# A split-precision decoder kernel: three products of 288 columns per contraction step and half, replaced for the first 256 tokens by one product of 512 columns and one of 256

## The reference, cut to what matters

```
x  -> mixer -> y;   h = x + rmsnorm(y @ w_out) * g_mix_post
u  = rmsnorm(h) @ w_ffn_up                     # 1024 -> 5632
c  = depthwise causal conv of width 3 over u
y  = (gelu(gate) * val) @ w_ffn_down           # 2816 -> 1024
h  = h + rmsnorm(y) * g_ffn_post
h  = h + rmsnorm(sigmoid(h @ w_ple_gate) * (p @ w_ple_proj)) * g_ple
```

## Time and profile before

| | |
|---|---|
| median of 3 runs | 2083.34 us (2082.45 to 2084.76) |
| the profiled execution's own time | 2080.89 us |
| its span | 2079.1 us |
| PE busy | 1912.2 us, 92% |
| DVE busy | 1131.7 us, 54% |
| ACT busy | 717.4 us, 35% |
| mean granted TensorE clock | 0.937 |

### The profile page before, as it was taken

The page is one execution under the profiler, slowest core; times in us unless marked ns, Lnnn a source line. Parts: engine busy times, 40 slices in busy tenths (PEclk is TensorE's granted clock), DMA queues, the critical chain, the costliest instruction groups (busy, mean ns, idle before and its releaser), DMA issues.

```text
span 2079.1 us, 34106 instructions
## 1 busy us (share of the span) xinstructions
PE 1912.2 (92%) x13244; PEld 1660.8 (80%) x13244; DVE 1131.7 (54%) x2433; ACT 717.4 (35%) x1300; POOL 13.7 (1%) x27
## 2 busy tenths in 40 slices
PE   6999889899999979999999898787799999979997
PEld 5587555798999979988489896344598999979987
DVE  7982154547777762253322395555557777762254
ACT  3211233454333342254322222444454333342252
POOL 0000000000000000000000000000000000000000
PEclk9999878899999999999999957799999999999998
DMA  4112457512222222131122310655212222222121
GB/s 165 62 43 86 159 175 275 198 42 71 92 81 81 68 102 81 55 114 62 44 88 82 110 48 10 238 205 201 82 48 72 87 86 81 68 97 83 56 81 46
DMA packets 77851, 204.12 MB, mean 98 GB/s; under 512 B 12530, under 2 KB 14754, under 8 KB 77218
## 3 DMA queue, kind: packets, MB, share of 16 engines
q1 hardware_dynamic: 75442, 189.70, 27.0%
q0 software_dynamic: 2288, 12.72, 1.7%
HBM read 190.81 MB, written 10.40 MB: 97 GB/s over the span
## 4 chain that ended last, share of the span: by engine, by line
PE 83%; DVE 12%; ACT 3%; issue 2%; DMA 1%; DVEq 0%; POOL 0%; ACTq 0%; POOLq 0%
PE psum L395 39%; PE psum L559 12%; PE psum L1491 6%; PE psum L403 5%; PE psum L2034 3%; PE psum L1235 2%; PE psum L790 2%; PE psum L1210 1%; PE psum L481 1%; PE psum L1328 1%; PE psum L1305 1%; PE psum L2175 1%; DVE sb_arena_r L355 1%; PE psum L495 1%; PE psum L1060 1%
## 5 line engine op out<-in xcount | busy, mean ns | idle before, releaser
L395 PE MATMUL psum<-sb_a_sb_r,sb_ring_r 128*128 128x288 f32 x1280 | 259.1, 295 | 0.0
L395 PE MATMUL psum<-sb_a_sb_r,sb_arena_r 128*128 128x288 f32 x1280 | 257.0, 296 | 0.0
L395 PE MATMUL psum<-sb_y_sb_r,sb_arena_r 128*128 128x288 f32 x704 | 207.1, 294 | 11.4 <-DVE sb_arena_r L355 11.2
L395 PE MATMUL psum<-sb_y_sb_r,sb_ring_r 128*128 128x288 f32 x704 | 208.6, 296 | 0.0
L395 PEld LDWEIGHTS psum<-sb_a_sb_r,sb_ring_r 128*128 128x128 f32 x1280 | 206.8, 188 | 0.0
L395 PEld LDWEIGHTS psum<-sb_a_sb_r,sb_arena_r 128*128 128x128 f32 x1280 | 204.2, 188 | 0.0
L355 DVE TENSOR_TENSOR sb_ring_r<-sb_ring,sb_ring_r 128x1024 fp32r<-128x1024 f32 (+1 forms) x78 | 101.6, 1306 | 159.6 <-ACT sb_ring_r L352 158.9
L352 ACT ACTIVATE sb_ring_r<-sb_ring 128x1024 fp32r<-128x1024 f32 (+1 forms) x78 | 87.4, 1124 | 286.3 <-PE psum L395 221.2
L559 PE MATMUL psum<-sb_arena_r 128*128 128x288 f32 x960 | 160.7, 302 | 8.3 <-DVE sb_arena_r L355 8.3
L395 PE MATMUL psum<-sb_arena_r,sb_ring_r 128*128 128x288 f32 x1056 | 145.4, 299 | 20.9 <-DVE sb_arena_r L355 20.9
L395 PEld LDWEIGHTS psum<-sb_arena_r,sb_ring_r 128*128 128x128 f32 x1056 | 143.6, 192 | 21.3 <-issue 21.3
(11 more groups left out here) (420 smaller groups left out, 3415.4 us busy)
## 6 DMA issues: line engine op xcount, KB each, us to landing
sb_ring<-w SPq DMA_DIRECT2D x166, 512.0 KB, 3.5
sb_ring<-wd SPq DMA_DIRECT2D x32, 704.0 KB, 4.1
sb_arena<-sb_v SPq DMA_DIRECT2D x64, 256.0 KB, 5.4
sb_arena<-moba_v SPq DMA_DIRECT2D x56, 256.0 KB, 5.0
sb_ring<-moba_k SPq DMA_DIRECT2D x32, 256.0 KB, 4.1
sb_a_sb<-moba_k SPq DMA_DIRECT2D x32, 256.0 KB, 5.4
sb_ring<-sb_k SPq DMA_DIRECT2D x32, 256.0 KB, 4.0
sb_a_sb<-sb_k SPq DMA_DIRECT2D x32, 256.0 KB, 5.4
```

Source lines behind the costliest of these rows:

```text
L395: ins = e.eng.matmul(out[:, half, :], fr(w[p][:, k, :]), fr(x[q][:, k, cols]), start=(first and k == 0 and i == 0), stop=(last and k == kb ...
```

## The change

For each k, the tokens are cut at 256 in place of 288 (`CA`, `CW`, `COLS`). For the first 256 tokens the high and the low part of the activations are read together by one product of 512 columns with the high weights, which fills one bank: its left 256 columns hold high weights x low tokens, its right ones high x high. One product of 256 columns then adds low weights x high tokens to the right half. The other 320 tokens keep their three products, now of 320 columns. So a step of all tokens is five products in place of six, with 512 + 256 + 3 x 320 = 1728 columns, as 6 x 288 = 1728 before. ScalarE copies the right part of the bank out, and VectorE adds the left part (`dve_add_low`, and a line in `dve_up`); this addition now frees the tile. Where ScalarE took squares or a sigmoid straight from PSUM, it takes them for these tokens from SBUF behind that addition.

```diff
+CA = 256
+CW = (CA, T - CA)
-        a_sb = sb2("a_sb", KD * T)
-        y_sb = sb2("y_sb", KD * T)
+        ya_sb = sb2("ya_sb", 2 * KD * T)
+        y_sb, a_sb = ya_sb[:, 0:KD * T], ya_sb[:, KD * T:2 * KD * T]
+        def mm_first(e, bank, w, both, k, begin, end):
+            c = COLS[0]
+            wide = lambda: e.eng.matmul(psum[:, bank, :].rearrange("p (q n) -> p q n", q=2), fr(w[0][:, k, :]),
+                                        fr(both[:, :, k, c]), start=begin, stop=end)
+            low = lambda: e.eng.matmul(psum[:, bank, CA:2 * CA], fr(w[1][:, k, :]), fr(both[:, 1, k, c]),
+                                       start=False, stop=False)
+            if end:
+                low()
+                return wide()
+            wide()
+            return low()
+        def mm_second(e, bank, w, both, k, begin, end):
+            for i, (p, q) in enumerate(((0, 1), (0, 0), (1, 1))):
+                ins = e.eng.matmul(psum[:, bank, 0:CW[1]], fr(w[p][:, k, :]), fr(both[:, q, k, COLS[1]]),
+                                   start=(begin and i == 0), stop=(end and i == 2))
+            return ins
+        def mm_tokens(e, s, w, both, kb, first=True, last=True, x_parts=None, per=1):
+            for k in range(kb):
+                if x_parts is not None:
+                    e.eng.wait_ge(xl_ready, x_parts + per * (k + 1))
+                mm_first(e, 2 * s, w, both, k, first and k == 0, last and k == kb - 1)
+                ins = mm_second(e, 2 * s + 1, w, both, k, first and k == 0, last and k == kb - 1)
+            return ins
+        def act_high_out(e, dst, src):
+            e.eng.activation(dst, src, ACT.Copy).then_inc(high_out, 1)
+        def dve_add_low(e, t, dst, src):
+            e.highs += 1
+            e.eng.wait_ge(high_out, e.highs)
+            e.eng.tensor_tensor(dst, dst, src, ALU.add).then_inc(copied["dve"], 1)
...
         def act_up(e, acc):
-                        act.activation(u[:, 2:2 + HALF], psum[:, 2 * s, 0:HALF], ACT.Copy)
-                        act.activation(u[:, 2 + HALF:2 + TP], psum[:, 2 * s + 1, 0:TP - HALF], ACT.Copy)
+                        act.activation(u[:, 2:2 + TP], tokens(s)[:, 0:TP], ACT.Copy)
...
         def dve_up(e, acc, layer):
-                        v.wait_ge(copied["act"], c0 + 2 * j + w + 1 + i * RING)
+                        v.wait_ge(high_out, c0 + 2 * j + w + 1 + i * RING)
+                        v.tensor_tensor(u[:, 2:2 + CA], u[:, 2:2 + CA], psum[:, 2 * ((n0 + 2 * j + w) % 4), 0:CA], ALU.add)\
+                            .then_inc(copied["dve"], 1)
+                        v.wait_ge(copied["dve"], d0 + 2 * j + w + 1 + i * RING)
...
         def act_down(e, acc, buf):
                 wait_filled(e, t)
-                act_part_square(e, [halves(z) for z in buf], m, pair(t.s))
-                e.eng.activation(halves(a[:, m, :]), pair(t.s), ACT.Copy).then_inc(copied["act"], 1)
+                act_high_out(e, a[:, m, :], tokens(t.s))
+                e.eng.wait_ge(*t.out)
+                act_part_square(e, buf, m, a[:, m, :])
...
         def dve_layer_end(e, acc, layer):        # the gate sweep
-            for j in range(2):
+            for j in range(4):
+                dve_sweep_first(e, t[f"A{j}"], j)
+                if j < 2:
+                    dve_slab(e, gate_pairs[4 + 2 * j], 2 * j)
                 product(j, 0)
-                if j:
-                    dve_part_sum(e, gate_sums[0], 1)
-                dve_slab(e, gate_pairs[4 + 2 * j], 2 * j)
-                dve_slab(e, gate_pairs[5 + 2 * j], 2 * j + 1)
+                if j < 2:
+                    dve_slab(e, gate_pairs[5 + 2 * j], 2 * j + 1)
+                if 1 <= j < 3:
+                    dve_part_sum(e, gate_sums[0], j)
```

More of the change, by code:

```diff
@@ L439, in dve_norm, with sums @@
                 e.eng.scalar_tensor_tensor(dst[:, k, :], src[:, k, :], vcol(layer, gain, k), rstd[:, :], ALU.mult, ALU.mult)
-        COLS = (slice(0, HALF), slice(HALF, T))
-        def sums(at):
-            return [cut(at + i * T, T) for i in range(3)]
+        COLS = (slice(0, CA), slice(CA, T))
+        def sums(at, half):
+            return [cut(at + 2 * i * CW[half], 2 * CW[half]) for i in range(3)]
         def sweep_tiles(acc, pre):
             order = ["A0", "A1", "A2", "A3", "B0", "nA", "B1", "B2"] + (["pA"] if pre else []) + ["B3"]
-            return {x: acc.next("act") for x in order}
+            return {x: acc.next("dve" if x[0] == "A" else "act") for x in order}
         def act_rstd(e, t, cols, ready=None):
@@ L551, in dve_split_half, with mm_half @@
             e.parts += KD
-        def mm_half(e, out, w, x, half, x_parts=None, ks=range(KD)):
+        def mm_half(e, bank, w, both, half, x_parts=None, ks=range(KD)):
             for k in ks:
@@ L557, in mm_half @@
                     e.eng.wait_ge(xl_ready, x_parts + k + 1)
-                for i, (p, q) in enumerate(((0, 0), (0, 1), (1, 0))):
-                    ins = e.eng.matmul(out, fr(w[p][:, k, :]), fr(x[q][:, k, COLS[half]]),
-                                       start=(k == 0 and i == 0), stop=(k == KD - 1 and i == 2))
+                ins = (mm_first, mm_second)[half](e, bank, w, both, k, k == 0, k == KD - 1)
             return ins
@@ L570, in pe_sweep_unit @@
                     e.eng.wait_ge(wl_ready, e.splits)
-                last = mm_half(e, psum[:, 2 * t.s + i, 0:HALF], pairs[m], x, half, e.parts if m == 0 else None)
+                last = mm_half(e, 2 * t.s + i, pairs[m], x, half, e.parts if m == 0 else None)
             last.then_inc(acc_ready, 1)
@@ L1483, in pe_dense_split @@
                 e.eng.wait_ge(wl_ready, e.splits)
-                t = acc.next("act")
+                t = acc.next("dve")
                 wait_emptied(e, t)
-                for k in range(KD):
-                    if m == 0:
-                        e.eng.wait_ge(xl_ready, e.parts + 2 * k + 2)
-                    for half in range(2):
-                        for i, (p, q) in enumerate(((0, 0), (0, 1), (1, 0))):
-                            last = e.eng.matmul(pair(t.s)[:, half, :], fr(split[(m + off) % 4][p][:, k, :]),
-                                                fr(x[q][:, k, COLS[half]]), start=(k == 0 and i == 0),
-                                                stop=(k == KD - 1 and i == 2))
-                last.then_inc(acc_ready, 1)
+                mm_tokens(e, t.s, split[(m + off) % 4], both, KD, x_parts=e.parts if m == 0 else None, per=2)\
+                    .then_inc(acc_ready, 1)
             e.parts += 2 * KD
@@ L1499, in act_dense_split @@
             n0 = acc.n
-            for m in range(tiles):
+            done = [None] * tiles
+            for m in range(tiles + 1):
                 if m + AHEAD < tiles:
                     act_split_slab(e, m + AHEAD, n0 + m + AHEAD - 3 if m + AHEAD >= 4 else None, off)
-                t = acc.next("act")
-                wait_filled(e, t)
-                e.eng.activation(halves(dst(m)), pair(t.s), func(m)).then_inc(copied["act"], 1)
-        def dve_dense_split(e, tiles):
-            for m in range(AHEAD, tiles):
-                dve_split_slab(e, m)
+                if m < tiles:
+                    t = acc.next("dve")
+                    done[m] = t.out
+                    wait_filled(e, t)
+                    act_high_out(e, dst(m), tokens(t.s))
+                if m and func(m - 1) is not ACT.Copy:
+                    e.eng.wait_ge(*done[m - 1])
+                    e.eng.activation(dst(m - 1), dst(m - 1), func(m - 1)).then_inc(func_done, 1)
         def sp_split_first(ld):
@@ L1529, in pe_up @@
             late = acc.next("act")
-            n0, c0, w0 = acc.n, acc.count["act"], e.splits
+            n0, c0, w0 = acc.n, acc.count["dve"], e.splits
+            held = [acc.last[(n0 + j) % 4] for j in range(4)]
             def tiles(i, count):
@@ L1689, in pe_down @@
                     e.eng.wait_ge(wl_ready, e.splits)
-                    x = [z[:, 11 * part:11 * part + 11, :] for z in (ffh, ff)]
-                    last = mm_split(e, pair(t.s), dsplit[part], x, 11, first=(part == 0), last=(part == 1),
-                                    x_parts=e.parts + 11 * part if m == 0 else None)
+                    last = mm_tokens(e, t.s, dsplit[part], f_both[:, :, 11 * part:11 * part + 11, :], 11, first=(part == 0),
+                                     last=(part == 1), x_parts=e.parts + 11 * part if m == 0 else None)
                     last.then_inc(part_done if part == 0 else acc_ready, 1)
@@ L1795, in act_gate_square @@
             e.eng.wait_ge(prod_ready, e.prods)
[L1796 to L1797 removed]
+            act_part_square(e, [two(z) for z in gate_sums[half]], j, a[:, 2 * j:2 * j + 2, COLS[half]])
             if j == 3:
@@ L2120, in dve_proj_c @@
                 dve_split_slab(e, n, off=2)
+            dst = [z[:, m, :] for z, n in ((qh, 4), (kh, 4), (gh, 4), (zqk, 8)) for m in range(n)]
             for m in range(20):
```

188 lines of the change are left out of this document (108 added, 80 removed).

## The result

The changed kernel takes **2092.16 us** (median of 20 runs, 2081.93 to 2098.88), the kernel before 2084.82 us beside it (20 runs, 2080.23 to 2095.05): a ratio of 1.0035, 95% interval 1.0022 to 1.0048. It is slower by 7.3 us, where the forecast was 0.5% faster, and it lies just above the upper end of the range (2092). None of the 20 runs lies between 2089.94 and 2094.38, so the median is the middle of a gap between two groups of ten runs. The profiled execution took 2098.88 us, the longest of its 20 runs; that of before took 2080.89, near its shortest. So the 17.6 us between the two spans (2096.7 and 2079.1) are more than the change is worth, and a part of what follows is to find out which part.

A forecast was written before the change was run, and what follows sets the result against it. The prediction took TensorE's split products, 132.7 ns each, to bound the kernel. From 2080.9 us it took 18.7 gained, added 8.2 lost to reach 2070.4, and, as that execution was 2.4 below the median, forecast 2072.8 us, range 2033 to 2092.

The forecast's parts named there:

- what a product costs: Split products on TensorE: 12.7 ns extra paid per product, so five instead of six gain 18.7 us over 1472 steps.
- R1: Split products: the extra goes with the columns, a step saves 0 to 2.6 ns, 2087 to 2091 us; chance 0.25.
- The narrow product: Split product of 256 columns in each step: 119.4 ns taken, 132.7 the upper end, where the gain is gone.
- (a): Fence between up and down products: the addition stands before the convolution, 0.5 us, in two layers 1.0.
- (b): Head of the gate sweep: TensorE arrives earlier and only waits longer, 3.4 us; VectorE's chain grows, 1.6 us.
- (c): Switch into the up product: VectorE's second-half operations 32 columns wider, 0.4 us with the norm, twice 0.8.
- (d): End of the projection: the addition comes between ScalarE's copy and the fence, once 0.5 us.
- (e): Tail of the kernel: closing operations on a half that is 32 columns wider, 0.9 us.
- R5: Up product: VectorE frees tiles too late and TensorE waits before them, 2080 to 2110 us; chance 0.04.
- R2: Split products: weight-load floor near 133 ns, hidden by wider products, 756.3 ns a step, 2033 us; chance 0.13.
- R3: Split products: token and weight reads share one supply, 767.9 ns a step, 2050 us; chance 0.12.
- R4: New product shapes are slow: 2092 us with the narrow at 132.7 ns, 460 us more in plain form; chance 0.08.

The follow-up runs named there:

- e1: Kernel before with 896 more split products at its very end, results unread, in series of equal width; 131.7 ns a product at 288 columns, 233.5 at 512.
- e8: Changed kernel with every VectorE addition cut to two columns, waits and order kept; 2095.56 us, ratio 1.0058.
- e0: Changed kernel again, unedited; 2090.39 us, ratio 1.0024.
- the controls: Kernel before with 8, 24 or 64 unneeded split products added in layer 1's projection; 2088.69, 2088.64 and 2094.96 us.

## Why the prediction was wrong

**The step that failed** is the one on what a product costs: "One load per product makes that a price per product. I take 12.7 ns per product." The 12.7 ns were real, but they are a lower rate of streaming: between 288 and 512 columns e1 has 0.8 ns fixed and 0.454 ns a column, and at 288 columns neither half the weights nor unchanged ones take any of it away. That is rival R1 (0.25). Its "A step then saves 0 to 2.6 ns" falls a little short of the 3.6 ns saved in the up product, and its time, 2087 to 2091, lies one microsecond below the result. The reason given for setting it lower was that the low clock showed 8 ns on 240 in place of 12.7 on 120. That was misread, too: the starts behind that wait lie 378 ns apart once and then 240 ns, 18 times, so the 8 ns are the first step's, and at the low clock there is no extra at all. Neither a price per column nor one per product was visible there, so the stretch could not speak against R1 alone. Every split product in the trace had the same width, 288, so nothing there could tell a price per product from one per column. A second width was what was missing, and the earlier trace rows had it only for another type.

**The narrow product** was named the uncertain one. It came out at 117.4 ns in the up product, a little under the forecast 119.4. What was off by the most was the wide one, 231.9 against 226, and the 320, 147.8 against 146.0 three times a step. In sum 792.7 ns in the up product against 783.5.

**What was gained.** Up product 254.81 - 253.67 = 1.1 us a layer, down product -0.45 a layer, projection 0.6: 2 us in these, and, if the other 320 steps (out and gate sweeps, the up product's first four slabs) saved 3.6 ns each, 1.2. About 3 us in place of 18.7. e1 by itself would give a loss of 3 ns a step (793.6 against 790.2); within the kernel a product of 288 columns takes 1 ns more than in e1, a wide one 1.6 and a narrow one 2.6 less. That difference is open.

**The losses** were right in place and size. From the last product before a wait to the first behind it, after less before: (a) the fence 11.12 - 10.72 = 0.4, twice 0.8 (1.0 forecast). (b) The head of the gate sweep 5.89 - 3.99 = 1.9, and 1.15 - 0.74 = 0.4 at the first tile, twice 4.6 (3.4 + 1.6). (c) The switch 5.78 - 5.40 = 0.4, twice 0.8 (0.8). (d) The projection's end 1.65 - 1.12 = 0.5 (0.5). (e) The tail, from the last layer's closing plain products to the end, 0.85 (0.9). Sum 7.5 us, 8.2 forecast. VectorE's additions in the up product took 422 ns each (430 forecast), with VectorE waiting for ScalarE before them in places; they cost nothing there, and e8 bears that out. R5 did not happen.

**The other rivals.** R2 (a weight load of 133 ns) fell with e1: 120.0 ns for 256 columns, 111.7 for 128. R3 (one supply for tokens and weights) had 512 columns at 215.9 ns, and they take 233.5; with half the weights 288 columns are no faster, and 512 are by 2 ns. R4 did not happen: two pieces cost nothing.

**The sum again.** 7.5 lost and 3 gained are 4.5 us slower, which is the direction and the greater part of the result. Measured are 7.3 (4.6 to 10.0 by the interval), and 5.0 in e0 (1.7 to 8.3). The medians of the controls add 1 to 3 us for a shift, which would make 5.5 to 7.5. The prediction had allowed for it in its last sentence ("a clock that falls at other places than before could move the time by 2 us either way"), but as noise about zero. The part by shift is argued from the three controls, none of them clear of noise by itself, the jumps and the low-clock times, and is not isolated: no run holds the clock still. The same holds for the switch into the up product, where TensorE's x96 run takes 16.61 us in the changed kernel though 96 x 147.8 ns are 14.2, and 14.58 before, though 96 x 132.7 are 12.7: 0.5 us more in the layer. Behind the wait the clock stays low longer than before, as windows of before and then of after show (columns as above):

```profile
475.00:480.00 5.00, 4.80 (x24) 4.80 (x25) 2.91 (x12) 0.25 (x1) 0.00 (x0) 0.66 0.00 0
```
```profile
475.00:480.00 5.00, 5.00 (x19) 5.00 (x20) 2.86 (x11) 0.00 (x0) 0.00 (x0) 0.50 0.00 0
```

## What to carry to other kernels

When a pitch is above its streaming time and all instructions have one width, the trace can't say whether the rest is paid per instruction or per column; a change that only merges instructions rests wholly on that, so measure a second width first. Merging at equal columns had small change to offer here (6 ns of 799 a step, of which an uneven cut took 2.5 back), while work that moved from a covered place to the engine that TensorE waits for was paid nearly in full (0.4 us more at the fence for an addition of 0.42). The time was at the wait: closing one stall of 3.7 us in each layer, by order alone, brought 0.6%, more than the merge could have brought.

## What the runs showed of the hardware

- Between 288 and 512 columns, split products (rounded float32, fp32r) stream at 0.454 ns a column at the full granted clock, bf16 at 0.417. 288 columns take 131.7 and 122.5 ns, 512 take 233.5 and 216.
- For fp32r there is a floor of 111.7 ns, the same for 128 and for 224 columns, and 256 columns take 120.0; bf16 with 128 columns went at 55.8. What sets the floor no run shows.
- At the low clock split products take their columns at 1.2 a ns and nothing more: 240 ns from start to start for 288 columns in the kernel before, 213, 267 and 427 for 256, 320 and 512 in the changed one.
- At 288 columns the time does not depend on the partitions used (64 or 128), the columns of weights (64 or 128), whether the weights change, or on one or two banks; at 512 it does not depend on whether the tokens lie in two pieces, and with 64 columns of weights it is 231.4 ns, against 233.5.
- A stretch with the same instructions took 305 to 317 us in different versions of the kernel, and with it 127 to 154 us at the low clock. In the three controls products that nobody needs moved the median by 1 to 3 us, up to 0.13%, beyond their own length, so here a difference of that size can't be put down to the instructions that were changed.
